# Stick-breaking attention in a three-block kernel: both heads of a pair at one query block, on the two halves of the array

## What is computed

```
z = einsum('bhtd,bhsd->bhts', qb, kb) * scale          # scores
log_beta = log_sigmoid(z)
log_one_minus = where(causal, log_sigmoid(-z), 0)
tail = cumsum(log_one_minus, reverse) - log_one_minus
weights = masked_exp(causal, log_beta + tail)
out = einsum('bhts,bhsd->bhtd', weights, vb)           # values
```

## Time and profile before

| | us |
|---|---|
| median of 3 runs | 2875.94 (2874.59 to 2878.57) |
| profiled execution, its time | 2878.48 |
| profiled execution, its span | 2877.2 |
| TensorE busy | 2759.1 (96% of the span) |
| VectorE busy | 1676.3 (58%) |
| ScalarE busy | 1294.0 (45%) |
| stage 1, from the first scores at 56.9 to those of stage 2 at 180.2 | 123.3 |
| stage 2, from there to the next mixer's first multiplication at 304.6 | 124.4 |

### The profile page before, as it was taken

One profiled execution on the slowest core, in us unless ns is written; L12 is line 12 of the kernel. 1 busy time (PEld: TensorE's weight loads), 2 busy tenths in 40 slices (PEclk: granted clock), 3 DMA queues, 4 the chain that ended last, 5 costly groups with the idle time before them and its releaser, 6 DMA issues.

```text
span 2877.2 us, 52600 instructions
## 1 busy us (share of the span) xinstructions
PE 2759.1 (96%) x21304; PEld 2192.8 (76%) x21304; DVE 1676.3 (58%) x3155; ACT 1294.0 (45%) x2359; POOL 223.5 (8%) x281
## 2 busy tenths in 40 slices
PE   8999999999998999999999999999898899999998
PEld 6766777778886777777777777777888778778876
DVE  3555656574457535655555565766576664652566
ACT  4344534333234645555556444344454344542234
POOL 0000000000000011111001003355400000000000
PEclk9999999999999999999999999999999999999999
DMA  3110111123344552323333325446744374421124
GB/s 130 30 37 30 45 45 45 43 67 119 105 154 132 181 156 68 92 69 90 90 90 91 99 103 161 131 157 229 246 141 155 127 266 130 161 86 44 37 66 154
DMA packets 186210, 316.60 MB, mean 110 GB/s; under 512 B 78048, under 2 KB 116208, under 8 KB 184176
## 3 DMA queue, kind: packets, MB, share of 16 engines
q1 hardware_dynamic: 185968, 313.23, 34.4%
HBM read 239.19 MB, written 73.99 MB: 109 GB/s over the span
## 4 chain that ended last, share of the span: by engine, by line
PE 78%; DVE 13%; ACT 5%; issue 2%; DMA 2%; DVEq 0%; SPq 0%; ACTq 0%
PE ps L261 20%; PE ps L263 18%; PE ps L262 18%; PE ps L2738 5%; PE ps L2444 3%; PE ps L2470 2%; PE ps L2457 2%; DVE wparts L346 2%; PE ps L871 2%; ACT wparts L333 1%; PE ps L845 1%; PE ps L819 1%; DVE mk__59 L3102 1%; DVE h L1479 1%; DVE ST L3135 1%
## 5 line engine op out<-in xcount | busy, mean ns | idle before, releaser
L261 PE MATMUL ps<-xs,wparts 128*128 128x512 f32 (+1 forms) x1664 | 699.5, 420 | 10.9 <-DVE xs L1587 9.2
L263 PE MATMUL ps<-xs,wparts 128*128 128x512 f32 (+1 forms) x1664 | 655.4, 394 | 0.0
L262 PE MATMUL ps<-xs,wparts 128*128 128x512 f32 (+1 forms) x1664 | 654.2, 393 | 0.0
L346 DVE TENSOR_TENSOR wparts<-wring,wparts 128x1024 fp32r<-128x1024 f32 (+1 forms) x256 | 314.5, 1229 | 291.8 <-ACT wparts L333 266.3
L261 PEld LDWEIGHTS ps<-xs,wparts 128*128 128x128 f32 (+1 forms) x1664 | 313.0, 188 | 131.9 <-issue 68.1
L333 ACT ACTIVATE wparts<-wring 128x1024 fp32r<-128x1024 f32 (+1 forms) x256 | 269.7, 1054 | 296.2 <-PE ps L263 188.3
L263 PEld LDWEIGHTS ps<-xs,wparts 128*128 128x128 f32 (+1 forms) x1664 | 312.8, 188 | 72.3
L262 PEld LDWEIGHTS ps<-xs,wparts 128*128 128x128 f32 (+1 forms) x1664 | 314.0, 189 | 55.8 <-issue 1.9
L2548 ACT ACTIVATE Pm<-Pm,ml 128x128 f32<-128x128 f32 (+1 forms) x384 | 168.2, 440 | 112.3 <-DVE ml L2619 112.0
L2619 DVE CUSTOM_DVE_ANT_0 Pm<-ps,mask 128x128 f32<-128x128 f32 (+1 forms) x384 | 110.9, 349 | 177.2 <-PE ps L2444 177.1
L2392 POOL COPY perm<-qkg 128x1024 f32<-128x1024 f32 x32 | 63.4, 2016 | 1464.4 <-ACT qkg L382 1194.0
(11 more groups left out here) (417 smaller groups left out, 4909.4 us busy)
## 6 DMA issues: line engine op xcount, KB each, us to landing
wring<-in_wo SPq DMA_DIRECT2D x96, 512.0 KB, 3.5
ops<-rw SPq DMA_DIRECT2D x32, 640.0 KB, 6.3
wring<-in_w SPq DMA_DIRECT2D x39, 512.0 KB, 3.6
wring<-in_w2a SPq DMA_DIRECT2D x29, 512.0 KB, 6.0
wring<-in_w2u SPq DMA_DIRECT2D x28, 512.0 KB, 4.2
wring<-in_wg SPq DMA_DIRECT2D x24, 512.0 KB, 3.9
wring<-in_w2v SPq DMA_DIRECT2D x24, 512.0 KB, 3.7
MB<-wst SPq DMA_DIRECT2D x48, 256.0 KB, 5.3
```

The costliest lines, as they stand in the source:

```text
L261: nc.tensor.matmul(out, a, c, start=start, stop=False)
L262: nc.tensor.matmul(out, b, c, start=False, stop=False)
L263: return nc.tensor.matmul(out, a, d, start=False, stop=stop)
L346: K.nc.vector.tensor_tensor(W.part(i, 1), W.raw(i), W.part(i, 0).bitcast(F32), ALU.subtract).then_inc(*K.dve.done("w_lo", W.first + i))
```

## The change

An item becomes a pair P: both heads of the pair at one query block. There are 8 pairs for each stage, in the order of blocks 4, 5, 6, 7, 0, 1, 2, 3. Index h replaces N % 2 in `B.be`, `B.nb`, `B.pr` and `B.wt`, so the two buffers hold the two heads of one block. Scores of head 0 and head 1 are written alternately, and so are their values. The ring `B.sb_s` gets four banks in place of three, `B.sb_o` one in place of two. The weights of one head are now in a function, `sb_weights`. A pair takes six steps on each engine:

| step | TensorE | ScalarE | VectorE |
|---|---|---|---|
| 0 | scores, both heads | sigmoids, head 0 | |
| 1 | | sigmoids, head 1 | weights, head 0 |
| 2 | values of the pair before, both heads | | gate product of the pair before, if due |
| 3 | | | weights, head 1 |
| 4 | transposes, head 0 | copy, head 0 | copy, head 0 |
| 5 | transposes, head 1 | copy, head 1 | copy, head 1 |

```
-    B.sb_s, B.sb_o = Ring(K, K.banks[3:6]), Ring(K, K.banks[6:8])
+    B.sb_s, B.sb_o = Ring(K, K.banks[3:7]), Ring(K, K.banks[7:8])
...
-SB_ORDER = [(h, i) for g in (4, 0) for h in range(2) for i in range(g, g + 4)]
+SB_ORDER = (4, 5, 6, 7, 0, 1, 2, 3)
...
+            banks = {}
+            for h in range(2):
+                for c, _ in enumerate(sb_chunks(i)):
+                    banks[h, c], old = B.sb_s.take(("s", P, h, c), ("nb", P, h, c))
+                    if old:
+                        pe.wait_ge(*(yield old))
             for c, (c0, w) in enumerate(sb_chunks(i)):
...
+                for h, r in enumerate(RH):
+                    nc.tensor.matmul(banks[h, c][:, 0:w], q[r, half(i, 128)], k[r, c0:c0 + w], start=True,
+                                     stop=True).then_inc(*pe.done("s", P, h, c))
             yield STEP
...
+            for h in range(2):
+                for c, _ in enumerate(sb_chunks(i)):
+                    pe.wait_ge(*(yield "tv_act" if c else "tv", P - 1, h, c))
             for j in range(i + 1):
-                a = nc.tensor.matmul(ob[r, half(i % 4, 128)], v[:, j, r], B.wt[:, N % 2, half(j, 128)],
-                                     start=(j == 0), stop=(j == i))
-            a.then_inc(*pe.done("av", N))
+                for h, r in enumerate(RH):
+                    a = nc.tensor.matmul(ob[r, half(i % 4, 128)], v[:, j, r], B.wt[:, h, half(j, 128)],
+                                         start=(j == 0), stop=(j == i), skip_group_check=True)
+            a.then_inc(*pe.done("av", P - 1))
...
+        for h in range(2):
+            if P:
+                act.wait_ge(*(yield "t", P - 1, h, len(sb_chunks(sb_block(P - 1))) - 1))
```

More of the change, by code:

```diff
@@ L646, in blocks, with sb_block @@
     return x.rearrange("p (n b) -> p n b", b=2 << lev)
-SB_ORDER = [(h, i) for g in (4, 0) for h in range(2) for i in range(g, g + 4)]
-def sb_block(N):
-    return SB_ORDER[N % 16]
+SB_ORDER = (4, 5, 6, 7, 0, 1, 2, 3)
+def sb_block(P):
+    return SB_ORDER[P % 8]
 def sb_chunks(i):
@@ L809, in sb_pe @@
     v = cells(v)
[L810 to L813, removed]
+    for m in range(9):
+        P = 8 * p + m
+        if m < 8:
+            i = sb_block(P)
             pe.wait_ge(*(yield "uev", 4 * p + 1, 1))
-            for c, (c0, w) in enumerate(sb_chunks(i)):
[L816 to L820, removed]
-            yield STEP
[L822 to L832, removed]
+            banks = {}
[4 more added lines that the diff above has]
+                        pe.wait_ge(*(yield old))
+            for c, (c0, w) in enumerate(sb_chunks(i)):
+                for h, r in enumerate(RH):
+                    nc.tensor.matmul(banks[h, c][:, 0:w], q[r, half(i, 128)], k[r, c0:c0 + w], start=True,
+                                     stop=True).then_inc(*pe.done("s", P, h, c))
+            yield STEP
             yield STEP
-        if 0 <= n - 2 < 16:
-            h, i = sb_block(n - 2)
-            r, N = half(h, 64), 16 * p + n - 2
+        if m > 0:
+            i = sb_block(P - 1)
             if i % 4 == 0:
-                ob, old = B.sb_o.take(("av", N + 3), ("sb_y", N + 3))
+                ob, old = B.sb_o.take(("av", p, i // 4), ("sb_y", p, i // 4))
                 if old:
@@ L966, in b1_pe @@
     yield from weave(sb_pe(K, B, 1), in_turn(hgrn_units_pe(K, B, 0), gates_pe(K, B, range(2, 4))))
-    pe.wait_ge(*(yield "sb_y", 31))
+    pe.wait_ge(*(yield "sb_y", 1, 0))
     yield from weave(rec_pe(K, B, 0), in_turn(hgrn_units_pe(K, B, 1), gates_pe(K, B, range(4, 7))))
@@ L1066, in hgrn_units_act @@
     if p:
-        act.wait_ge(*(yield "av", 31))
+        act.wait_ge(*(yield "av", 15))
     for h in range(2):
@@ new lines, in sb_dve @@
+    for m in range(9):
+        P = 8 * p + m
+        if m < 8:
+            yield STEP
+            yield from sb_weights(K, B, P, 0)
+            yield STEP
+        if m > 0 and sb_block(P - 1) % 4 == 3:
+            g = sb_block(P - 1) // 4
+            y = B.yT[:, p, half(g)]
+            dve.wait_ge(*(yield "av", P - 1))
+            dve.wait_ge(*(yield "uev", 4 * p + 3, 1))
+            dve.in_order()
+            nc.vector.tensor_tensor(y, K.bank["av", p, g], y, ALU.mult).then_inc(*dve.done("sb_y", p, g))
+        yield STEP
+        if m < 8:
+            yield from sb_weights(K, B, P, 1)
+            yield STEP
+            w = min(512, 128 * (sb_block(P) + 1))
+            for h in range(2):
+                dve.wait_ge(*(yield "t", P, h, 0))
+                if P:
+                    dve.wait_ge(*(yield "av", P - 1))
+                dve.in_order()
+                nc.vector.tensor_copy(B.wt[:, h, 0:w], K.bank["t", P, h, 0][:, 0:w]).then_inc(
+                    *dve.done("tv", P, h, 0))
+                yield STEP
```

121 lines of the change are left out of this document (56 added, 65 removed).

## The result

| | before | after | forecast |
|---|---|---|---|
| median, us | 2875.88 | 2845.44 (2842.08 to 2850.28) | 2842 (2830 to 2861) |
| profiled execution, time and span | 2878.48, 2877.2 | 2850.28, 2849.0 | 2844.2 |
| stage 1 | 123.3 | 105.2 | about 105 |
| stage 2 | 124.4 | 113.1 | about 109 |

The change makes the kernel faster by 1.1%: the ratio of the times is 0.989, with an interval of 0.9873 to 0.9908. The first four executions of the changed kernel spread over 8 us, and the profiled one is their slowest; a second set of four (experiment 5) has the median 2846.3. One execution of all, the profiled one of experiment 6, took 6252.8 us, with the multiplications of L261 at 844 ns in the mean where the kernel after has 418, and is left out.

What follows compares the result with a forecast made beforehand. TensorE was taken to bound both stages. Work 193.3, waits 6.1 + 10.6 and clock dips 3.4 give 213.4 us against 247.7, 34.3 less; from the median 2875.9 that forecasts 2842, range 2830 to 2861.

Steps and rivals of the forecast that it cites:

- Work: TensorE in both stages: full overlap saves 31.0 us, half as many visits 11.4; work falls from 235.7 to 193.3.
- the other 12.0 are waits and two stretches at the lower clock: Both stages before the change: prices explain 235.7 of 247.7 us; the remainder was taken as no work.
- Waits: TensorE waiting in the wide blocks, mostly for VectorE's weights and copies: 6.1 us in stage 1, 10.6 in stage 2.
- the gate's clip: Stage 2, block 5: VectorE's forget-gate line, ahead of head 1's weights, delays their end from 10.7 to 12.5: 1.8 us.
- The cause given for the 0.7 at block 4: Both stages: a split between weights and copies delays the next scores, which need all four banks: 0.7 us each.
- Clock: TensorE in the stages: two dips to 1.2 GHz instead of 2.4, as before the change, costing 3.4 us together.
- Everything behind the stages moves forward unchanged: Rest of the kernel after both stages: keeps its length and only starts earlier; no change in size.
- VectorE's chain bounds the pairs: Rival: each of 8 wide pairs waits 2 us more, 16 us and one dip: 2860; chance 0.18.
- The Trainium skill's rule: Tiling doesn't speed up emptying PSUM, which may bound; alone, it loses the columns' 31.0 us, keeps 11.4: 2864.
- The waits don't come: Rival: the present 12.0 us cover the stages' new waits, so the whole 42.4 is gained: 2833; chance 0.11.
- The halves don't overlap: Rival: scores and values gain only the visits' 11.4 us, and waits grow by 8: 2872; chance 0.04.
- Slower: Rival: each of 16 pairs is a closed loop waiting 4.3 us, 69 in all: 2894; chance 0.05.

Runs made afterwards that it cites:

- experiment 5: The changed kernel run and profiled once more, nothing altered (source of the second profile); 2846.3 us, ratio 0.9890.
- experiment 6: Changed kernel with the units' split on VectorE moved by one step, sooner or later; 2837.5 us, ratio 0.9863; its profiled execution was disturbed.
- experiment 4: Changed kernel with the two mask lines of each head's weights applied twice; 2860.6 us, ratio 0.9931.
- 10: Changed kernel with both mask lines of each head's weights left out; 2838.2 us, ratio 0.9863.
- experiment 8: Changed kernel with both the units' splits and stage 2's forget gate moved; 2837.1 us, ratio 0.9857.
- experiment 11: Changed kernel with only the units' splits moved, the same kernel as experiment 6 run again; 2838.8 us, ratio 0.9864.
- 7: Changed kernel with only stage 2's forget gate moved, its logarithm behind the sigmoids of block 6; 2839.0 us, ratio 0.9863.
- experiment 2: Changed kernel with only the scores written head after head; 2846.3 us from a single execution.
- experiment 3: Changed kernel with only the values written head after head; 2845.2 us from a single execution.
- experiment 9: Changed kernel with the two heads' scores in separate steps, a unit's slice between them, values still in turn; 2851.5 us, ratio 0.9912.
- 12: Kernel of experiment 8 with the values written head after head; 2839.8 us, ratio 0.9871.

## Why the prediction was right

The forecast of 2842 lies 3.4 under the median. By its own steps:

**Work.** 42.4 less was forecast, 43.4 went (42.9 by the second profile). Full overlap of both forms was taken from the two other places of the kernel, and holds. The absolute figure was 193.3, measured 194.6 and 195.1; the step "the other 12.0 are waits and two stretches at the lower clock" was wrong in its split. Windows give before 6.3 of idle time and 3.4 of clock, so 2.3 of the 12.0 was work that the prices had missed, and 1.3 to 1.8 of that stayed.

**Waits.** 16.7 was forecast, 16.9 measured, block by block:

| | forecast | measured |
|---|---|---|
| stage 1, block 4 | 3.0 + 0.7 | 1.84 + 1.06, + 0.97 |
| block 5 | 0 | 0 |
| block 6 | 0.3 | 0.23 |
| block 7 | 2.1 | 2.05 |
| stage 2, block 4 | 0.5 + 0.7 | 0.96 + 0.97 |
| block 5 | 1.8 + 1.2 | 1.72 + 1.19 |
| block 6 | 4.3 | 0.94 + 2.99 |
| block 7 | 2.1 | 2.03 |
| narrow blocks | 0 | 0 |

A sum of row durations along one pair's chain (scores, sigmoids, both heads' weights, what stands between) was good to 0.7 us for each block. The links inside stage 2 came out as closely: the gate's clip was put at 8.0 us after the scores of block 5 and the sigmoids of block 6 at 19.7, and they started at 8.1 and 19.7 (183.04 and 194.62 less 174.97). Experiments 4 and 10 show the chain as the cause, 8 and 11 the split's part at block 7, and 7 the gate's at blocks 5 and 6. The total is a little better than its parts: blocks that waited more than forecast (0.7 at block 4 of stage 2) and less (0.4 at block 6) cancel in part. One detail fell out differently: the waits at block 4 of stage 1 and block 6 of stage 2 are partly at head 0's transposes, where the prediction put all at head 1's. The cause given for the 0.7 at block 4 wasn't shown.

**Clock.** Two stretches were forecast, "as now". In the first profile there were three, one twice as long, and 3.4 us more; this is the larger part of the 4.9 us by which the stages missed 213.4 (work is 1.3 of it, waits 0.2). In the second profile there were two, and its time, 2844.5, is the forecast of 2844.2. The term was too low by 3.4 in one execution and right in another. The agreement of that time is in part luck: its stages took 215.4, 2.0 over the forecast, and the rest of the kernel was 1.7 shorter than in the profile of before.

**Outside the stages.** "Everything behind the stages moves forward unchanged": 2877.2 - 247.7 = 2629.5 before, 2849.0 - 218.3 = 2630.7 after. In the eleven profiles of the experiments other than that of 6 this rest lies between 2624 and 2632, though nothing in it was changed, so a difference of a few us between the times of two kernels says less than their stages do.

**The rivals.** *VectorE's chain bounds the pairs* was priced at 2 us more for each wide pair, and no block came out so. The Trainium skill's rule, "TensorEngine Tiling (Array Packing)", PSUM Bottleneck, would have taken back the whole 31.0 of the columns; the idle time took back 10.6. Nor is it the emptying of PSUM in the narrow sense: the waits for the copies are 3.1 of the 16.9 us, those for the weights ahead of them 13.8, with the split, the gate and late sigmoids that delayed the weights. *The waits don't come* fell with the same row. *The halves don't overlap* fell with the 1.92 and 1.90 us. *Slower* needed 3.2 us of wait for each pair; the mean is 1.1, and the narrow blocks have none.

**What the prediction did not see** is how the gain is shared out. It summed work and waits for the changed kernel and was right with the sum, but a reader might have taken the 15.7 us of the values' columns as 15.7 us of time. Put back alone, 9.8 us of the values' work found 4.0 us of waits to run in, and 21.4 of the scores' found 9.1; with the stretches at the low clock that were missing from these profiles, the stages grew by 4.1 and 8.9. The last part of the work removed came out of stretches in which TensorE would have been early for its transposes.

## What to carry to other kernels

Before removing work from a bound engine, sum the chain of one iteration on the other engines from row durations, with everything that stands between its links; that sum, less what the bound engine still has to do between the same two points, is the wait, and once there is a wait, further work removed between them is worth nothing. Then look at what stands inside the chain without belonging to it (here a unit's split and a forget gate): moving both by a few steps gave another 9 us without removing an instruction. And read in the trace that an experiment did what it says before reading its time: the order written for the scores was no switch for their overlap.

## What the hardware showed beside this

**Neighbours in the queue overlap even when not in turn.** Scores written head after head, at most four instructions a head, overlap fully (experiment 2). Values of block 7, 16 instructions a head, overlap at the seam alone. The starts of single instructions in experiment 3, in us from the group's start, head by head as their spacing tells them apart:

```
head 0: 0.00 0.16 0.27 0.38 ... 1.36   then 1.47 1.58 1.69
head 1:                         1.37 1.53 1.64 1.75 1.85 ... 3.06
```

Head 1 starts with three of head 0's 16 instructions still to come, and both then go in pairs. The same holds for the smaller groups of the stages (us that the values hold TensorE, experiment 3 against the kernel after):

| instructions a head | 2 | 4 | 6 | 8 | 10 | 12 | 14 | 16 |
|---|---|---|---|---|---|---|---|---|
| head after head | 0.37 | 0.59 | 1.07 | 1.51 | 1.95 | 2.38 | 2.82 | 3.26 |
| in turn | 0.37 | 0.58 | 0.81 | 1.02 | 1.25 | 1.46 | 1.68 | 1.90 |

Up to four a head the order makes no difference, and each instruction beyond costs 0.11 to 0.13; with eight a head, too, head 1 starts with three of head 0's still to come. Over both stages the differences sum to the 9.8 us of work that experiment 3 put back. The reading that fits is that TensorE takes an instruction for the other half of the array past about three that wait for their own half. The rows of the trace don't name the head, so the spacing and the table are the evidence for it, and no run tested it by itself. A slice of full-array work between the heads ends the overlap (experiment 9).

**The low clock is not a fixed price.** Stretches at 1.2 GHz of 3.4 us, and once of 6.8, each began during one of TensorE's waits or within 1.5 us of its end. But waits of the same length also passed without: 2.98 us at block 6 in experiment 11, 2.1 at block 5 in experiment 8 and 3.3 at block 7 of both stages in experiment 4 left the clock at its full level. A wait of 2 us or more in these stages cost sometimes its length and sometimes 1.7 to 3.4 more. The sum of the idle time doesn't tell it either: experiments 12, 9 and 8 (7.2 to 9.7 us idle) and 11 (14.2) had no such stretch in the stages, but the kernel before had two with 6.3, behind waits of 0.9 and 1.3. What decides between the two isn't shown.
